# The ninth modulation unit moved behind the attention, the tenth behind the merge, in the first two layers

## What is computed

```python
for l in range(DEPTH):                                   # 2 layers
    mod = c_act @ ada_w[l] + ada_b[l]                    # 1024 x 6144
    sh1, sc1, g1, sh2, sc2, g2 = jnp.split(mod, 6, axis=-1)
    xm = modulate(rms_norm(x, norm_mix_w[l]), sh1, sc1)
    q, k, v, u_pool, ga, gp = jnp.split(xm @ w_in[l], splits, axis=-1)
    # q, k: norm per head and rotary; attention, pooling
    attn = gqa(q, k, v) @ w_attn_o[l]
    pool = multiscale_pool(u_pool, ...) @ w_pool_o[l]
    merged = sigmoid(ga) * attn + sigmoid(gp) * pool
    x = x + g1 * (merged @ w_out[l])
    xf = modulate(rms_norm(x, norm_ffn_w[l]), sh2, sc2)
    x = x + g2 * peer_ffn(xf, ...)                       # gathers of expert rows
```

## Time and profile before

| | us |
|---|---|
| median of 3 runs | 3308.18 (3300.7 to 3309.91) |
| the profiled execution, its own time | 3308.17 |
| its span, first to last instruction | 3306.4 |
| PE busy | 2331.6 (71%) |
| DVE busy | 2124.3 (64%) |
| ACT busy | 937.5 |
| POOL busy | 1008.6 |
| mean granted TensorE clock | 0.832 |

### The profile page before, as it was taken

One profiled execution on the slowest core, in us unless ns is written; L12 is line 12 of the kernel. 1 busy time (PEld: TensorE's weight loads), 2 busy tenths in 40 slices (PEclk: granted clock), 3 DMA queues, 4 the chain that ended last, 5 costly groups with the idle time before them and its releaser, 6 DMA issues.

```text
span 3306.4 us, 35194 instructions
## 1 busy us (share of the span) xinstructions
PE 2331.6 (71%) x12383; PEld 1716.8 (52%) x12383; DVE 2124.3 (64%) x4418; ACT 937.5 (28%) x1483; POOL 1008.6 (31%) x1044
## 2 busy tenths in 40 slices
PE   4997444454335996444454235899999999999898
PEld 3855222222003755222222003689879978987797
DVE  6865876677756865777677754655555565556654
ACT  2411111011002411111111003444554444445543
POOL 0101766667771102766667770000000000000000
PEclk9998666767667998666777667899999997999899
DMA  8763999999997754999999994245425432554253
GB/s 323 268 228 137 406 407 407 408 409 409 405 405 278 285 210 150 407 407 407 407 409 410 401 409 165 89 153 195 178 102 179 179 139 81 193 186 153 103 191 126
DMA packets 311815, 892.92 MB, mean 270 GB/s; under 512 B 22424, under 2 KB 31616, under 8 KB 311552
## 3 DMA queue, kind: packets, MB, share of 16 engines
q0 software_dynamic: 147456, 536.94, 40.9%
q1 hardware_dynamic: 164224, 354.32, 30.0%
HBM read 890.13 MB, written 1.05 MB: 270 GB/s over the span
## 4 chain that ended last, share of the span: by engine, by line
PE 45%; DMA 15%; POOL 13%; issue 13%; DVE 11%; ACT 2%; SPq 1%; DVEq 0%; POOLq 0%; ACTq 0%
DMA proj<-in_expert_u,eidx 13%; PE lin L754 8%; PE lin L755 8%; PE lin L756 8%; POOL proj L2392 7%; POOL vbuf L2405 3%; POOL ring L2405 3%; PE lin L724 3%; DVE proj L2106 2%; PE psT L756 2%; PE psT L755 2%; PE psS L755 2%; PE psS L756 2%; PE psT L754 2%; PE psS L754 2%
## 5 line engine op out<-in xcount | busy, mean ns | idle before, releaser
L2106 DVE CUSTOM_DVE_ANT_0 proj<-proj,psT 128x1024 f32<-128x1024 f32 x512 | 615.3, 1219 | 354.9 <-DMA proj<-in_expert_u,eidx 333.8
L1667 DVE TENSOR_TENSOR weights_split<-ring,weights_split 128x1024 fp32r<-128x1024 f32 (+1 forms) x376 | 450.4, 1207 | 376.2 <-ACT weights_split L1467 373.8
L2392 POOL DMA_INDIRECT proj<-in_expert_u,eidx x512 | 485.6, 948 | 575.3 <-DVEq L2080 321.1
L1467 ACT ACTIVATE weights_split<-ring 128x1024 fp32r<-128x1024 f32 (+1 forms) x376 | 391.5, 1046 | 467.7 <-PE lin L756 291.5
L1030 PE MATMUL psS<-const,pT 128*128 128x16 f32 x64 | 18.8, 373 | 423.5 <-DVE pT L2093 390.9
L1043 PE MATMUL lin<-ring,rowb 128*32 128x512 f32 x896 | 167.7, 786 | 207.4 <-DMA pr<-in_expert_v,pT 140.7
L754 PE MATMUL lin<-weights_split,xT_high 128*128 128x512 f32 (+1 forms) x736 | 297.8, 405 | 11.1 <-DVE xT_low L1716 5.1
L756 PE MATMUL lin<-weights_split,xT_high 128*128 128x512 f32 (+1 forms) x736 | 288.9, 393 | 0.0
L1043 PE MATMUL lin<-vbuf,rowb 128*32 128x512 f32 x1024 | 183.1, 869 | 131.2 <-DVE rowb L2133 131.2
L1410 ACT ACTIVATE gel<-hdot 128x16 f32<-128x16 f32 x32 | 6.9, 216 | 927.4 <-DVE hdot L2106 927.4
L2405 POOL DMA_INDIRECT vbuf<-in_expert_v,pT x256 | 239.9, 937 | 78.1 <-issue 76.9
(11 more groups left out here) (279 smaller groups left out, 4982.3 us busy)
## 6 DMA issues: line engine op xcount, KB each, us to landing
ring<-in_mlp_w_up SPq DMA_DIRECT2D x32, 2048.0 KB, 8.7
ring<-in_mlp_w_down SPq DMA_DIRECT2D x32, 2048.0 KB, 7.7
ring<-in_w_in SPq DMA_DIRECT2D x16, 2048.0 KB, 9.9
ring<-in_w_query SPq DMA_DIRECT2D x16, 2048.0 KB, 18.4
vbuf<-in_ada_w SPq DMA_DIRECT2D x12, 2048.0 KB, 13.6
ring<-in_diff_w_in SPq DMA_DIRECT2D x12, 2048.0 KB, 8.1
ring<-in_ada_w SPq DMA_DIRECT2D x8, 2048.0 KB, 12.6
ring<-in_moba_w_in SPq DMA_DIRECT2D x6, 2048.0 KB, 7.9
```

The lines of the kernel that those rows point to most:

```text
L1467: act.activation(part(p, 0, kind, w), raw_piece(slot, p, kind, w), ACT.Copy).then_inc(hi_ready, 1)
L1667: dve.tensor_tensor(part(p, 1, kind, w), raw_piece(slot, p, kind, w), part(p, 0, kind, w).bitcast(F32), ALU.subtract).then_inc(lo_ready, 1)
L2106: dve.tensor_tensor_reduce(ubuf[:, n % GB, :], ubuf[:, n % GB, :], x_row, 1.0, 0.0, ALU.mult, ALU.add, hdot[:, cb, k:k + 1]).then_inc(h_re ...
L2392: pool.indirect_dma_start(out=ubuf[:, (16 * cb + k) % GB, :], out_offset=None, in_=table["u"], in_offset=bass.IndirectOffsetOnAxis(ap=eidx ...
```

## The change

Unit ada 9 leaves its place ahead of the attention. Its 2 MB go to slot 3 of `ring` behind `("w", 0)`, and `("w", 1)`, which had that slot, is loaded after it once ada 9's sums on DVE are done. On DVE ada 9 stands between `tr_all` and mix 0; on PE `ada_sum(9)` stands ahead of k = 0 of `o` 1, and both mix sums move from k = 2 to k = 4 behind a wait for mix 1. `mod_columns(1, ...)` is split: `ffn_columns` (one operation, ahead of the attention) and `ffn_scale` (three, between mix 0 and mix 1). Unit ada 10 moves on DVE from ahead of `merge(1)` to behind `merge(3)`; its gate row and ada 11 move behind the first residual. `ada_sum(10)` and `ada_sum(11)` stand ahead of k = 0 and k = 6 of `w` 1. GpSimd's code is the same.

```diff
-                (("ada", 9), 3), (("in", 7), 1)])
-LATER_UNITS = [(("o", 0), 0), (("o", 1), 1), (("w", 0), 2), (("w", 1), 3), (("ada", 10), 0), (("ada", 11), 1)]
+                (("in", 7), 1)])
+LATER_UNITS = [(("o", 0), 0), (("o", 1), 1), (("w", 0), 2), (("ada", 9), 3), (("w", 1), 3), (("ada", 10), 0), (("ada", 11), 1)]
...
 SP
-                ada(9, *summed(7))
...
                 unit(("w", 0), cols_of(T["w_out"][l], 0, UC), lin_done, 8)
-                unit(("w", 1), cols_of(T["w_out"][l], UC, UC))
+                ada(9)
...
                 mix_load(0, pv_done, GQA.nout)
                 mix_load(1, pv_done, GQA.nout)
+                unit(("w", 1), cols_of(T["w_out"][l], UC, UC), *summed(9))
                 mix_load(2, acc_ready, SUM_AT["mix", 0] + 1)
...
 PE
                 gqa_columns(C, 8)
                 gqa_columns(C, 0)
-                ada_sum(9)
...
                 def first_mixes(k):
-                    if k == 2:
+                    if k == 0:
+                        ada_sum(9)
+                    if k == 4:
+                        pe.wait_ge(acc_ready, SUM_AT["mix", 1] + 1)
                         mix_sum(0)
                         mix_sum(1)
 
                 def last_sums(k):
-                    if k == 2:
+                    if k == 0:
+                        ada_sum(10)
+                    if k == 6:
                         ada_sum(11)
...
                 def first_merged(k):
                     if k == 0:
                         mix_sum(2)
-                        ada_sum(10)
...
 DVE
+            def ffn_columns():
+                dve.wait_ge(s_ada, SUM_AT["ada", 8] + 1)
+                link(dve.tensor_tensor(modc[:, 24:36], psS[:, 0, 24:36], pcol[:, 24:36], ALU.add))
+            def ffn_scale():
+                dve.wait_ge(s_ada, SUM_AT["ada", 9] + 1)
+                link(dve.tensor_tensor(modc[:, 36:40], psS[:, 0, 36:40], pcol[:, 36:40], ALU.add))
+                link(dve.tensor_scalar(aff[:, 1, :], modc[:, 32:40], 1.0, None, ALU.add))
+                link(dve.tensor_tensor(aff[:, 1, :], aff[:, 1, :], pcol[:, 56:64], ALU.mult))
...
                 ada_unit(8)
-                ada_unit(9)
                 C.lin += 8
-                gqa_columns(C, GQA, 8)
-                gqa_columns(C, GQA, 0)
-                mod_columns(1, 56)
-                for b in (2, 4, 6):
+                for b in (8, 0, 2, 4):
                     gqa_columns(C, GQA, b)
+                ffn_columns()
+                gqa_columns(C, GQA, 6)
...
                 tr_all(C)
+                ada_unit(9)
                 next_mix_unit(0)
+                ffn_scale()
                 next_mix_unit(1)
...
                 merge(0)
                 next_mix_unit(2)
-                ada_unit(10)
                 merge(1)
                 merge(2)
+                merge(3)
+                ada_unit(10)
+                residual_unit(C, rowb[:, 0, :], 0)
                 gate_row(1, 0, psS[:, 1, :])
-                merge(3)
                 ada_unit(11)
-                residual_unit(C, rowb[:, 0, :], 0)
                 next_mix_unit(3)
```

More of the change, by code:

```diff
@@ L206 @@
 UNIT_AT = unit_table()
-FIRST_ADA = [("ada", n) for n in range(4, 10)]
+FIRST_ADA = [("ada", n) for n in range(4, 9)]
 INS1 = ["x", "c", "ada_w", "ada_b", "norm_mix_w", "w_in", "q_norm_w", "k_norm_w", "w_attn_o",
@@ L1847, in ada_unit @@
                 slot, landed = UNIT_AT["ada", n]
-                src = raw_unit(slot).rearrange("p (k n) -> p k n", k=KC)
+                src = raw_unit(slot).rearrange("p (k n) -> p k n", k=KC) if n < 9 else ring[:, slot, :, :]
                 if half != 1:
@@ L1860, in next_mix_unit, with mix_columns @@
                 partial_sums(ada_acc[:, q % 2, :], [mix_at[n % 2][k // 4][:, k % 4, :] for k in range(KC)], acc_ready)
[L1862 to L1871, removed]
+            def mix_columns():
+                link(dve.tensor_tensor(modc[:, 0:16], mix_sums[:, :], pcol[:, 0:16], ALU.add))
+                link(dve.tensor_scalar(aff[:, 0, :], modc[:, 8:16], 1.0, None, ALU.add))
+                link(dve.tensor_tensor(aff[:, 0, :], aff[:, 0, :], pcol[:, 48:56], ALU.mult))
+            def ffn_columns():
[6 more added lines that the diff above has]
+                link(dve.tensor_tensor(aff[:, 1, :], aff[:, 1, :], pcol[:, 56:64], ALU.mult))
             def gate_row(a, half, src):
@@ L1897, in _ @@
                 dve.wait_ge(p_col, 1)
-                mod_columns(0, 48)
+                mix_columns()
                 norm(C)
```

## The result

The changed kernel took 3315.65 us (median of 10 runs, 3307.85 to 3329.24), the kernel before 3307.55 (10 runs, 3300.27 to 3312.09): the medians are 8.1 us apart (ratio 1.0024). The ratio on record for these runs, which is not that of the two medians, is 1.0037 with a 95% interval of 1.0024 to 1.005, or 8 to 17 us. Either way the change makes the kernel slower, by an amount that the runs fix only roughly; 9.4 us were forecast. The runs of one kernel scatter over 12 to 21 us, and the execution that was profiled happens to be the second fastest of the ten, 3308.09 us with a span of 3306.3, hardly another span than that of before. So the spans of the two profiles say nothing about the change; its stage does.

A forecast was written before the change was run, and what follows sets the result against it. PE was taken as the bound behind the attention, DVE's added work free unless PE waits on it. Layers at +6.0 and +3.45 gave +9.45 on 3308.17, so 3317.6 us; range 3313 to 3322, with rivals 3307 to 3323.

The forecast's parts named there:

- The stall: In `o` 1 at the new wait, PE stands still until DVE finishes mix 1: 2.9 us a layer.
- Ada 9's sums in `o` 1: Four sums on PE ahead of k = 0 of `o` 1 make it end 0.9 us later a layer.
- The clock in the stall: Slow clock in `o` 1 from PE's wait costs a further 2.4 us a layer, range 0 to 3.05.
- The tail: Between the residuals DVE needs 15.8 us instead of 14.66, ending 1.15 us later; ada 10's sum leaves the path, 1.0.
- Ahead of the attention: Without ada 9 there, up to and including the first scores: gain 0.4 us in the first layer, 2.95 in the second.
- The sum: Whole kernel: +6.0 us in the first layer, +3.45 in the second, together +9.45.
- A stall with the clock up: Rival: PE stalls in `o` 1 but the clock stays up, +4.65 us, 3312.8 us; chance 0.2.
- Late loads: Rival: query weights and sub-keys arrive late, 3 to 5 us more a layer, 3322 to 3325 us; chance 0.08.
- DVE in time at mix 1: Rival: no wait in `o` 1, the kernel gets faster by 5 us, 3303 us; chance 0.05.
- Later slack: Rival: PE's wait is there but slack further on swallows it, 3308 to 3310 us; chance 0.1.

The follow-up runs named there:

- e1: Changed kernel with the wait and the two mix sums moved from k = 4 to k = 6 of `o` 1; ratio 0.9985 against the kernel before.
- e6b: Changed kernel with the wait and the mix sums back at k = 2, second execution; one run, 3444.30 us (before 3429.91 on that chip).
- e8: Changed kernel with the wait and the mix sums at k = 5; one run, 3436.11 us (before 3429.91 on that chip).
- c0: The changed kernel timed again without any edit; ratio 1.0036 against the kernel before.
- e3: Changed kernel with three unread products (2.6 us of PE work) ahead of the new wait; ratio 1.0006 against the kernel before.
- e4: Changed kernel with ada 10, ada 11, their gate rows and sums back where they were, only ada 9's part kept; one run, 3308.12 us.
- e2: Kernel before with only the ada 10, ada 11 and gate row part of the change, ada 9 unmoved; ratio 0.9997 against the kernel before.
- e7: e2 with `ada_sum(11)` behind the last `w` 1 product and both gate rows behind the second residual; ratio 0.9993 against the kernel before.

## Why the prediction was right

- **The stall.** Predicted 2.9 us a layer from DVE's three units and `ffn_scale` (the rows add up to 213.2 and not 213.3, so 2.8), measured 2.83 in both. `e1` removes it, `e6b` more than doubles it and `e8` cuts it to 1.12, the last two by the 1.72 us a step that PE does ahead of it. This step is shown.
- **Ada 9's sums in `o` 1.** 0.9 predicted, 0.81 measured (198.62 to 199.43).
- **The clock in the stall.** 2.4 us a layer, taken as four fifths of a row from elsewhere. In the profile it is 10.45 us from 209.37 to 219.82, against 1.70 for the sums at full clock and 6.87 for the records, so 1.9; in `c0` 3.5 (209.35 to 221.47 is 12.12). That the stall brings the clock down is shown by the eight layers in which it fell against the ten without a stall in which it did not; that less than 2.83 us can be enough is shown by `e8` and `e3`, and what decides there between the two layers is not. Its price is no fixed number: 1.9 to 3.6 for the same stall (3.6 in the first layer of `e4`), and the range of 0 to 3.05 was a little narrow at the top. One reading behind the number was wrong: in the second layer before, the clock fell at 1146.6 behind a single short idle time, the 1.11 us; the 0.94 us end at 1150.14, when it had long fallen. That makes the case for a fall in the new stall stronger, not weaker. The rule of the Trainium skill ("TensorE: Matmul & The Clock Gate", section "What's actually happening"), slow by default and released by activity, agrees with the falls to 0.50 behind these stalls. That rule does not say which of two equal stalls brings the clock down, and the section gives no price.
- **The tail.** 15.8 us between the residuals predicted, 15.91 measured. One term was off by little: ada 10's sum was priced at 1.0 us off the path, the stretch from the end of `o` 1 to the first residual shrank by 0.86 (218.13 to 249.31 before, 219.82 to 250.14 after). With it the stage sums to 0.81 + 2.83 + 1.9 + 1.25 - 0.86 = 5.9 us, against 6.06 measured and 6.4 predicted.
- **Ahead of the attention.** This is the step that was mis-sized: -0.4 and -2.95 us predicted, -1.8 and -2.1 measured (11.73 to 9.92; 10.49 + 19.58 to 9.91 + 18.08, up to the transposes of the attention rows, with the scores now at full clock). In the second layer the first score came 0.58 us earlier after ada 8's sums and not 2.2, since the clock fell ahead of it this time, and the sixteen score records gave back all of the 1.5 us and not half. The sum, -3.9 against -3.35, hides both; that is luck. I took the first layer's slow stretch as a property of that layer and left it in. It is none: the clock was at 0.50 there for 6.8 us in the first layer before and 3.4 after; `e1` had none of it in the first layer (8.34) and 6.8 us in the second (11.50), `e2` none in the first and 3.4 in the second. Without ada 9 the stretch takes 8.3, 9.9 or 11.5 us with 0, 3.4 or 6.8 us of slow clock in it; with ada 9, 9.9, 10.15 or 11.7 (`e2`, `e7`, before). So ada 9's unit costs 9.93 - 8.34 = 1.6 us there at full clock and 0.25 where the clock falls, and most of the 1.8 us won in the first layer is the clock's, not ada 9's.
- **The sum.** Two stages at +6.06 and -3.9 ahead are +8.2 us; the medians differ by 8.1, the forecast said 9.4. That the first two agree to 0.1 is luck too: the 8.2 come from one execution of each kernel, the same sum with `c0`'s rows is 15.4 - 5.5 = +9.9, and the interval on record is 8 to 17 us.
- **The rivals.** A stall with the clock up came true in one layer of `e8` and of `e3`, not in the changed kernel. Late loads: the sub-keys landed 9 us ahead of their use. DVE in time at mix 1, which would have made the kernel faster, is what `e1` brings about by moving PE, not DVE: the total went to 0.9985, as far as it can be told. Later slack: none, since in `e6b` all of the longer stall arrives in the stage.

## What to carry to other kernels

Work moved off an engine that waits, onto the same engine at a place where it is nearly level with the bound, has to be counted against the exact moment at which the bound asks for it: here three units of 5.9 us against sixteen us of products, 2.8 us short. The two mix sums stood two steps later at no cost and the whole stall was gone (`e1`); one step later left 1.12 us of it (`e8`). So try the place of the consumer before giving up the move. And where TensorE runs dense, a stall costs more than its length: here 2.83 us cost 4.8 to 6.5 us against `e1`, and 1.12 us cost 1.4 or 4.8. Price it with both clock levels and expect another price in every execution.

## What was not expected of the hardware

The granted clock ahead of the attention differs between executions and between the two layers of one program with the same instructions: 0, 3.4 or 6.8 us of slow clock in the same place. 0.26 us of stall before sixteen tiny products brought it down in one layer and not in the other (`e3`), 1.12 us cost 1.4 and 4.8 us (`e8`). In `e6b` the clock fell while TensorE stood still, in the changed kernel 1.6 and 1.8 us after it had started again. One execution ran at a mean of 0.62 (3946.82 us), at 0.65 where the others are at 1.00; another of the same kernel, on another chip, ran at 0.825, the other profiled ones at 0.817 to 0.834; what held the clock down is not known.
